# Moving the keys of an RWKV level from VectorE to GpSimd, and its transposed inverses from TensorE to a second stream transposition

## The reference

```python
def direction(xw, xa, d, reverse):
    w = rwkv_decay(xw, w0[d], w2[d])
    a = jax.nn.sigmoid(a0[d] + xa @ a2[d])
    k_d = k * (1 + (a - 1) * k_a)                       # the keys
    y = wkv7_scan(heads(r), heads(w), heads(k_d), heads(v), kk, heads(a), reverse)
    return y, k_d
# one step of wkv7_scan
    sa = jnp.einsum('bhvk,bhk->bhv', state, -kk_t)
    state = (state * w_t[:, :, None, :] + sa[..., None] * (kk_t * a_t)[:, :, None, :]
             + v_t[..., None] * k_t[:, :, None, :])
    y = jnp.einsum('bhvk,bhk->bhv', state, r_t)
# after both directions
k_bonus = 0.5 * (k_f + k_b)
bonus = jnp.sum(heads(r * k_bonus) * r_k, axis=-1, keepdims=True) * heads(v)
```

## Time and profile before

| | |
|---|---|
| median of 3 runs | 1865.01 us (1864.02 to 1874.56) |
| the profiled execution | 1870.9 us, span 1869.0 us, mean granted clock 0.937 |
| busy in the span | PE 89%, PEld 65%, DVE 54%, ACT 39%, POOL 15% |
| the chain that ended last | PE 57%, issue 26%, DVE 8%, ACT 4%, POOL 3% |
| RWKV rounds of layer 0 | 289 to 520 us |
| RWKV rounds of layer 1 | 1196 to 1427 us |

### The profile page before, as it was taken

The page is one execution under the profiler, slowest core; times in us unless marked ns, Lnnn a source line. Parts: engine busy times, 40 slices in busy tenths (PEclk is TensorE's granted clock), DMA queues, the critical chain, the costliest instruction groups (busy, mean ns, idle before and its releaser), DMA issues.

```text
span 1869.0 us, 28024 instructions
## 1 busy us (share of the span) xinstructions
PE 1658.8 (89%) x11272; PEld 1215.3 (65%) x11272; DVE 1007.3 (54%) x1533; ACT 732.3 (39%) x1201; POOL 289.2 (15%) x124
## 2 busy tenths in 40 slices
PE   2997875888998999989989978589889899999997
PEld 0784432666676888877757834256667688887885
DVE  6644458778217667754443244588752445445333
ACT  3434234566534233222243343456654432223223
POOL 1342000000032222211214410000002122222221
PEclk8898995999899999999989989789989999999999
DMA  7354110000043555443303310000002222232221
GB/s 293 129 165 159 33 55 35 2 2 2 2 147 107 198 197 183 180 157 135 121 16 124 91 68 1 0 2 2 2 2 91 68 90 90 90 103 99 77 103 68
DMA packets 34654, 163.00 MB, mean 87 GB/s; under 512 B 3841, under 2 KB 4097, under 8 KB 25857
## 3 DMA queue, kind: packets, MB, share of 16 engines
q1 hardware_dynamic: 34560, 161.65, 24.5%
HBM read 159.54 MB, written 2.10 MB: 86 GB/s over the span
## 4 chain that ended last, share of the span: by engine, by line
PE 57%; issue 26%; DVE 8%; ACT 4%; POOL 3%; DMA 1%; POOLq 0%; DVEq 0%; SPq 0%; ACTq 0%
PE bank L500 8%; PE bank L502 8%; PE bank L501 8%; PE bank_pair L500 3%; PE bank_pair L502 3%; PE bank_pair L501 3%; POOL work_parts L1923 2%; PE bank L547 2%; PE bank_pair L603 2%; PE bank L840 2%; PE bank L841 2%; PE bank L818 1%; PE bank L656 1%; PE bank L856 1%; POOL proj_weights_parts L1918 1%
## 5 line engine op out<-in xcount | busy, mean ns | idle before, releaser
L500 PE MATMUL bank<-work_parts,y_mix_parts 128*128 128x512 f32 x792 | 316.5, 400 | 21.5 <-DVE work_parts L1687 10.3
L502 PE MATMUL bank<-work_parts 128*128 128x512 f32 x792 | 316.0, 399 | 0.0
L1700 DVE TENSOR_TENSOR work_parts<-work,y_mix_parts 128x1024 fp32r<-128x1024 f32 x66 | 169.2, 2564 | 255.6 <-ACT y_mix_parts L970 255.6
L1918 POOL TENSOR_TENSOR proj_weights_parts<-proj_weights,proj_weights_hi_parts 128x1024 fp32r<-128x1024 f32 x54 | 130.4, 2419 | 936.1 <-ACT proj_weights_hi_parts L966 860.2
L1923 POOL TENSOR_TENSOR work_parts<-work,y_mix_parts 128x1024 fp32r<-128x1024 f32 x66 | 158.6, 2404 | 611.5 <-ACT y_mix_parts L970 611.5
L970 ACT ACTIVATE y_mix_parts<-work 128x1024 fp32r<-128x1024 f32 x132 | 133.0, 1054 | 261.7 <-DMA work<-mlp_dram 252.0
L501 PE MATMUL bank<-work_parts,y_mix_parts 128*128 128x512 f32 x528 | 208.8, 395 | 0.0
L500 PEld LDWEIGHTS bank<-work_parts,y_mix_parts 128*128 128x128 f32 x792 | 150.7, 190 | 58.8 <-issue 24.7
L502 PEld LDWEIGHTS bank<-work_parts 128*128 128x128 f32 x792 | 150.4, 190 | 36.0
L500 PE MATMUL bank<-work_parts,proj_weights_hi_parts 128*128 128x512 f32 x272 | 111.8, 411 | 25.3 <-DVE work_parts L1687 23.5
L501 PEld LDWEIGHTS bank<-work_parts,y_mix_parts 128*128 128x128 f32 x528 | 100.4, 190 | 24.4
(11 more groups left out here) (266 smaller groups left out, 3061.9 us busy)
## 6 DMA issues: line engine op xcount, KB each, us to landing
work<-mlp_dram SPq DMA_DIRECT2D x66, 1024.0 KB, 4.9
work<-ada_dram SPq DMA_DIRECT2D x64, 512.0 KB, 4.6
proj_weights<-tiles_dram SPq DMA_DIRECT2D x57, 512.0 KB, 3.6
x_res<-ada_dram SPq DMA_DIRECT2D x24, 512.0 KB, 4.9
x_res<-x_dram SPq DMA_DIRECT2D x2, 2048.0 KB, 10.6
mixer_inputs<-ada_dram SPq DMA_DIRECT2D x8, 512.0 KB, 17.5
work<-mlaw_dram SPq DMA_DIRECT2D x4, 640.0 KB, 4.4
out_dram<-x_res SPq DMA_DIRECT2D x8, 256.0 KB, 2.2
```

What stands on the lines that cost most here:

```text
L500: mm(out, w_hi, x_hi, start=start, stop=False)
L502: return mm(out, w_lo, x_hi, start=False, stop=stop)
L1700: TTT(MW_L[q][:, 1], MW_IN[q][:, 1], plain(MW_H[q][:, 1]), ALU.subtract).then_inc(msp_v.sem, msp_v.one("l1"))
L1918: pool.tensor_tensor(ring_l[s], ring[s], plain(ring_h[s]), ALU.subtract).then_inc(spl_q.sem, spl_q.one(f"t{s}"))
```

## The change

Four things change, all in the RWKV rounds.

1. `keys` and `bonus` leave DVE. They are six DVE instructions of 128x512 for a block; POOL now does them as seven, since the product with the constant and with the other tensor is split (kbs, kbk, kbr). POOL does them for all four blocks of a layer ahead of the last weight tiles. It starts a block as soon as ACT has made the factor f0.
2. `inverse_out` gets another stream transposition, step trans, that reads the 32 first partitions of `lane_inverse` and writes X0T directly. The 32 PE transposes of step X and their two ACT copies go.
3. On DVE the order is now trans, the ring of chunk 0, out.
4. On PE the order is T, Gram and values, Z, `rwkv_triangle(it + 1, 0)`, tokens. Z waits for step out as well. ACT copies T, then the diagonals, the state, Z and then the triangle.

```diff
-                      + [f"{n}{d}" for d in D2 for n in ("kd", "k")])
-        bon_v, bon_p = steps("bon_v", ["kbs", "kbr", "bon"]), steps("bon_p", ["BON"])
+                      )
+        key_q = steps("key_q", ["kd0", "k0", "kd1", "k1", "kbs", "kbk", "kbr"])
+        bon_v, bon_p = steps("bon_v", ["bon"]), steps("bon_p", ["BON"])
...
-                pe.wait_ge(inv_v.sem, inv_v.at("out", it))
-                for d in D2:
-                    for m in range(16 * d, 16 * d + 16):
-                        last = pe.transpose(PS[1 + d][0:32, (m % 16) * 32:(m % 16) * 32 + 32], XD[0:32, m, :], ident[0:32, 0:32])
-                    own(lev_p, last, f"X{d}")
-                scan_gram(it, 1)
-                scan_values(it, 0)
-                pe.wait_ge(lev_a.sem, lev_a.at("X1", it))
+                pe.wait_ge(inv_v.sem, inv_v.at("trans", it))
                 for i in range(16):
...
-                if early:
-                    rwkv_triangle(it + 1, 0)
+                scan_gram(it, 1)
+                scan_values(it, 0)
+                pe.wait_ge(inv_v.sem, inv_v.at("out", it))
                 pe.wait_ge(lev_a.sem, lev_a.at("T1", it))
...
+                if early:
+                    rwkv_triangle(it + 1, 0)
                 scan_tokens(it, b, 1)
...
+                own(inv_v, dve.transpose(X0T[0:32].rearrange("p m t -> p t m"), XL[0:32, 0:1024].rearrange("p (c i) -> p c i", c=32)), "trans")
+                scan_ring(it, 0)
                 own(inv_v, dve.transpose(XD[0:64].rearrange("p m t -> p t m"), XL[0:64, 0:1024].rearrange("p (c i) -> p i c", c=32)), "out")
...
+            def keys(it, b, d):
+
+                pool.wait_ge(pre_a.sem, pre_a.at(f"f{d}", it))
+                own(key_q, pool.tensor_tensor(KDD[d], LW[d], facing(mix(K0 + b), d), ALU.mult), f"kd{d}")
+                pool.wait_ge(key_q.sem, key_q.at(f"kd{d}", it))
+                if it % RB >= 2:
+                    pool.wait_ge(sc_p.sem, sc_p.at("Y", it - 2))
+                own(key_q, pool.tensor_tensor(BK[it % 2][d][:, :, 1, :], chunks(KDD[d]), chunks(PI[d]), ALU.mult), f"k{d}")
+                pool.wait_ge(key_q.sem, key_q.at(f"k{d}", it))
+
+            def bonus(it, b):
+
+                own(key_q, pool.tensor_tensor(KDD[0], KDD[0], KDD[1][:, ::-1], ALU.add), "kbs")
+                pool.wait_ge(key_q.sem, key_q.at("kbs", it))
+                own(key_q, pool.tensor_scalar(KDD[0], KDD[0], col(DR, b + DRV["r_kh"]), None, ALU.mult), "kbk")
+                pool.wait_ge(key_q.sem, key_q.at("kbk", it))
+                own(key_q, pool.tensor_tensor(KDD[0], KDD[0], mix(R0 + b), ALU.mult), "kbr")
+                pool.wait_ge(key_q.sem, key_q.at("kbr", it))
```

More of the change, by code:

```diff
@@ L1079, in level @@
                 for d in D2:
-                    act.wait_ge(lev_p.sem, lev_p.at(f"X{d}", it))
-                    own(lev_a, F(X0T[0:32, 16 * d:16 * d + 16, :], sixteen(PS[1 + d][0:32, :]), ACT.Identity), f"X{d}")
+                    act.wait_ge(lev_p.sem, lev_p.at(f"T{d}", it))
+                    own(lev_a, F(X0T[32:64, 16 * d:16 * d + 16, :], sixteen(PS[1 + d][64 * d + 32:64 * d + 64, :]), ACT.Identity), f"T{d}")
+                act.wait_ge(inv_v.sem, inv_v.at("out", it))
                 for q in range(2):
                     diagonal(it, q)
-                for d in D2:
-                    act.wait_ge(lev_p.sem, lev_p.at(f"T{d}", it))
-                    own(lev_a, F(X0T[32:64, 16 * d:16 * d + 16, :], sixteen(PS[1 + d][64 * d + 32:64 * d + 64, :]), ACT.Identity), f"T{d}")
                 scan_state(it, 0)
-                if early:
-                    triangle(it + 1, 0)
                 for e in range(2):
@@ L1093, in level @@
                     own(lev_a, F(XT[it % 2][rows, :, :, 32:64], PS[1 + e][rows, :].rearrange("p (d c t) -> p d c t", d=2, c=NCH), ACT.Identity), f"Z{e}")
+                if early:
+                    triangle(it + 1, 0)
             def scan_ring(it, s):
@@ L1467, in removals @@
                 own(pre_v, STT(B, B, -0.5, chunks(PI[d]), ALU.mult, ALU.mult), f"b{d}")
-            def keys(it, b, d):
-                dve.wait_ge(pre_a.sem, pre_a.at(f"f{d}", it))
-                own(pre_v, TTT(KDD[d], LW[d], facing(mix(K0 + b), d), ALU.mult), f"kd{d}")
-                dve.wait_ge(pre_v.sem, pre_v.at(f"kd{d}", it))
-                own(pre_v, TTT(BK[it % 2][d][:, :, 1, :], chunks(KDD[d]), chunks(PI[d]), ALU.mult), f"k{d}")
-            def bonus(it, b):
-                own(bon_v, TTT(KDD[0], KDD[0], KDD[1][:, ::-1], ALU.add), "kbs")
-                dve.wait_ge(bon_v.sem, bon_v.at("kbs", it))
-                own(bon_v, STT(KDD[0], KDD[0], col(DR, b + DRV["r_kh"]), mix(R0 + b), ALU.mult, ALU.mult), "kbr")
             def bonus_end(it, b):
@@ L1677, in rwkv_round @@
                     scan_ring(new, 1)
-                    if early:
-                        for d in D2:
-                            keys(new + 1, nxt + 1, d)
-                        bonus(new + 1, nxt + 1)
             def norm_rows(n, sc, sh):
@@ L1831, in _ @@
                     removals(l * RB, 0, d)
-                for d in D2:
-                    keys(l * RB, 0, d)
-                bonus(l * RB, 0)
                 for cur in range(-1, RB):
@@ L1924, in rest_mlp, with own @@
                     msp_q.sem, msp_q.one("l0"))
+            def own(s, ins, name):
+                ins.then_inc(s.sem, s.one(name))
+            def keys(it, b, d):
[13 more added lines that the diff above has]
+                pool.wait_ge(key_q.sem, key_q.at("kbr", it))
             for l in range(DEPTH):
@@ L1932, in _ @@
                 settle(pool, "pool")
+                pool.wait_ge(spl_q.sem, l * NTILE + NPROJ + 1 + (1 + 3))
+                for b in range(RB):
+                    for d in D2:
+                        keys(l * RB + b, b, d)
+                    bonus(l * RB + b, b)
+                pool.wait_ge(key_q.sem, key_q.at("kbr", l * RB + RB - 1))
                 for t in range(NPROJ + 2, NTILE):
```

15 lines of the change are left out of this document (8 added, 7 removed).

## The result

The changed kernel takes 1897.68 us (median of 4 runs, 1895.58 to 1897.95) against 1864.51 us of the kernel before on the same chip: ratio 1.0174 [1.0148, 1.0199] (the brackets hold the 95% interval, here and below), slower by 1.7%. The forecast was 1886 us, its range 1862 to 1899. The profiled execution took 1897.95 us, with a span of 1896.2 us and a mean granted clock of 0.928; that of before took 1870.9 us, so the traces have to account for 27.05 us.

A forecast was written before the change was run, and what follows sets the result against it. DVE bounds the stretch from the write-back transposition to the next inversion. 10 + 3.6 + 5.2 + 5.2 + 1.4 - 4.1 = +21.3 us on the 1865.0 us median gives 1886 us, range 1862 to 1899.

The forecast's parts named there:

- The mechanism: Ends of RWKV rounds: POOL takes turns with DVE's queries and removals; next inversion at 19.4 us instead of 14.2.
- The signs: In the changed profile: direction 0's queries and removals at 1.2 to 1.9 us instead of 0.68, beside POOL rows near 1.2.
- the first rival: Round ends: DVE keeps the port through back-to-back instructions, POOL enters only at its waits; +8 us, 1873 us, chance 0.17.
- the second: Rival, beside queries and removals: POOL and DVE do not collide, nothing is felt; -11 us, 1854 us, chance 0.15.
- The third: Rival, on PE: step X may be off the path where clock-keeping matmuls end late; no size or chance of its own.
- the last blocks: Last building round of each layer: without step X, T starts 2.06 us sooner; -4.1 us for the two layers.
- PE is free at about 16, before removals 1: PE at a round's end: direction 0's triangle, tokens and first chunk done about 16 us after the write-back transposition starts.
- The term of 15.4 us for four ends: Ends of rounds 0 and 1 in both layers: next inversion later by 3.6, 5.2, 5.2 and 1.4 us.
- 0 after round -1: End of round -1, both layers: no delay, since layer 0's distance was already 20.5 us with PE late.
- POOL's length: Each POOL instruction of 128x512: 1.2 us; bounds 1.2 to 2.4 for products, 0.6 to 1.2 with a single input.
- Ahead of the first rounds: Before each layer's first inversion: four POOL turns, with waits 5 us, delay DVE; +10 us for both layers.
- The clock: PE idle ahead of the triangle could drop the granted clock to 0.50 at four ends; up to 6 us more.

The follow-up runs named there:

- e2: The kernel before with only keys and bonus moved to POOL, step X and the old order kept: 1897.32 us, ratio to the kernel before 1.0158.
- e1: The changed kernel with keys and bonus back on DVE, new transposition and order kept: 1858.50 us, ratio to the kernel before 0.9969.
- e10: The changed kernel with the ring of chunk 1 moved ahead of direction 1's queries and removals on DVE: 1879.84 us, ratio to the kernel before 1.0084.
- e6: The changed kernel with bonus back on DVE, leaving four POOL instructions a block instead of seven: ratio to the kernel before 1.0086.
- e9: The changed kernel with two POOL products of a block done twice, nine POOL instructions instead of seven: ratio to the kernel before 1.0254.
- e5: The changed kernel with a block's four short DVE copies made by tensor_reduce over one element: 1892.71 us, ratio to the kernel before 1.0174.

## Why the prediction was right, and where it was not

- **The mechanism** was right: turns of POOL between DVE's queries and removals, and DVE late to PE. In the rounds nobody waited for POOL's own results but PE for the first bonus of a layer (2.2 us, where before the change it waited 1.6 us for DVE). The signs came out in part. Of the four products of direction 0 only the last removal took 1.64 us, one 0.85 and two 0.67; the turns fell on the two short copies, 1.23 us each. These copies are behind no wait, so the first rival (DVE keeps the port, ends of 16.9) is out, and e2 puts the second out (nothing felt, 1854 us; its own evidence against is two held DVE rows, not four). The third, that the change does less, is out by e1 and the last blocks. PE's idle time ahead of the first triangle was 2.4 us, not 5, with 2.0 us more ahead of the Gram matrix of chunk 2.
- **The size was short by a third, and that the time still fell inside the range is in part luck.** The sum had +21.3 us; the traces differ by 27.1 and the medians by 33.2. The upper end of the range stood on a lower clock and on longer POOL instructions; the largest part of what was missing came from neither, but from the next point.
- **The first miss, and the larger one: the step "PE is free at about 16, before removals 1".** DVE was sooner than I had it (removals 0 end at 10.4 after t0 instead of 11.65, removals 1 at 15.4 instead of 16.45). But on PE the triangle of direction 1 stands behind the Gram matrix of chunk 2, which needs the ring of chunk 1, and that stands behind removals 1 on DVE. I had read both orders and not put them together: a delay of DVE goes into PE's queue ahead of the triangle too. The triangle started at 18.2 instead of 16.7, and at the lower clock, and L1491 at 21.4 instead of 19.4. e10 takes this away and gives back 14.9 us over the six ends, 0.9% in the ratio: the 12.4 us of waiting for the ring, and in part the clock. Without it the ends are 18.6 us, less than the forecast's 19.4. The term of 15.4 us for four ends became 22.1.
- **The second miss: 0 after round -1**, measured +0.4 and +3.7 us. I had taken layer 0's 20.5 us as a property of this end; layer 1's was 17.6, which the prediction did not look at, and it became 21.3. With POOL's turns all six ends come to 20.7 to 21.5, whatever they were before: DVE's late removals and ring set them.
- **POOL's length** was 1.27 us, not 1.2, and 1.57 for the product with a constant, where I had bounded it by 1.2. By e6 and e9 each instruction costs about 1.2 us of an end. As an estimate, 0.07 us more for some five turns at six ends is 2 us.
- **Ahead of the first rounds** I had +10, measured +7.0 us: four DVE instructions were held, by 1.08, 1.06, 1.06 and 0.94 us (1.76, 1.23, 1.23 and 1.63 against 0.68, 0.17, 0.17 and 0.69) in layer 0, 4.1 us in all. What DVE's own keys had taken there before is gone, so that 3.5 us are left.
- **The last blocks** gave 7.3 us instead of 4.1, the rest being above all the clock in layer 0, above.
- **The second transposition** took 1.92 to 1.98 us instead of 2.05. The estimate of 1.07 us from the Trainium skill's Vector Engine (DVE) Microarchitecture Reference, section The reshape front-end and per-opcode configuration, doesn't fit; that of the row did.
- **The clock** was named as an upper cost of up to 6 us. It fell as foreseen, at the end of round 1 from 0.99 (431 to 437) to 0.50 (437 to 443), with the first triangle at 1.93 us; before the change PE had 1.00 there. The windows, before and changed:

```profile
427.00:433.00 6.00, 5.11 (x192) 4.30 (x188) 5.83 (x13) 4.87 (x11) 0.00 (x0) 1.00 0.01 4
```

```profile
437.00:443.00 6.00, 3.60 (x76) 2.91 (x76) 5.90 (x10) 2.21 (x5) 4.03 (x3) 0.50 0.00 0
```

The inversions' +2.6 us were not forecast, and I have not traced them; in e10, with the same POOL work, they are +0.5 us. Of the 32.7 us between the medians (1897.7 and 1865.0), 5.6 us are not in the traces compared: the profiled execution before was 5.9 us above its median, that of after 0.3.

## What to carry to other kernels

Work moved to POOL costs DVE about its own length once for each instruction that runs while DVE has products of two SBUF inputs or SBUF copies ready, however small that work is. With a single semaphore wait, the same work at a place where DVE reads PSUM, transposes, sums or waits cost nothing here but 2.1 us in the first inversion of a layer. When an engine is delayed, follow every queue of the engine that waits for it: here a 0.68 us step that stood behind the delayed work made half of the loss. Don't leave a small step that another engine needs soon behind work that becomes late.

## What the runs showed of the hardware

- A copy of 128x8, 0.17 us alone, is held until the POOL instruction of 128x512 beside it ends (1.22 to 1.25 us in the changed kernel); a tensor_reduce over one element with the same result is not (0.14 to 0.16 us in e5).
- Both sides wait: POOL's 1.27 us become 1.58 to 1.87 in the changed kernel, and 1.57 become up to 2.14.
- A stream transposition of 1024 elements takes 1.92 to 1.98 us with 32 partitions and 1.92 to 2.09 with 64 in the changed kernel: partitions hardly count.
- POOL's product of 128x512 takes 1.27 us, more than half of the 2.40 of 128x1024; with one input and a constant from memory it takes longer (1.57), not shorter.
